# Forgetting attention in 11 steps per head pair instead of 14

## The reference, cut to what matters

```python
def forgetting_attention(q, k, v, logf):
    """logit[t,s] = q_t.k_s/sqrt(d) + sum_{s<j<=t} log f_j, causal."""
    c = jnp.cumsum(logf, axis=1)
    ...
        s = jnp.einsum("bthd,bshd->bhts", qi, k).astype(jnp.float32) * scale
        s = s + (cqi[..., :, None] - c_k[..., None, :])
        s = jnp.where(kpos[None, :] <= qpos[:, None], s, -jnp.inf)
        p = jax.nn.softmax(s, axis=-1).astype(v.dtype)
        return jnp.einsum("bhts,bshd->bthd", p, v)
```

## Time and profile before

| | |
|---|---|
| runs before | 2881.91, 2880.11, 2880.3 us; median 2880.3 |
| span of the profiled execution, first to last instruction | 2879.8 us (its own time is not told apart from the runs; the median lies 0.5 us above this span) |
| mean granted TensorE clock | 0.989 |
| busy: PE, DVE, ACT, POOL | 2752.2, 1715.2, 1046.7, 936.7 us |
| attention part, first projection matmul after the phase before to first matmul of the next phase | 893.2 to 1552.4 us |

### The profile page before, as it was taken

The page is one execution under the profiler, slowest core; times in us unless marked ns, Lnnn a source line. Parts: engine busy times, 40 slices in busy tenths (PEclk is TensorE's granted clock), DMA queues, the critical chain, the costliest instruction groups (busy, mean ns, idle before and its releaser), DMA issues. The chain is left out here.

```text
span 2879.8 us, 39468 instructions
## 1 busy us (share of the span) xinstructions
PE 2752.2 (96%) x15534; PEld 2109.5 (73%) x15534; DVE 1715.2 (60%) x2674; ACT 1046.7 (36%) x1735; POOL 936.7 (33%) x549
## 2 busy tenths in 40 slices
PE   6999999999999999999999999979999999998999
PEld 5979797977778677777776887756666666666777
DVE  5787878785121344444445113766776777777586
ACT  4342534343110233233334002335666654444232
POOL 2232323232564121121221333543221144332465
PEclk9999999999999999999999999999999999999999
DMA  4141423233533111101112223521101111113544
GB/s 167 56 89 66 85 69 85 75 76 119 195 117 106 42 53 45 49 30 52 52 45 107 103 81 141 176 94 44 47 19 44 37 41 34 41 41 101 201 149 110
DMA packets 113751, 236.53 MB, mean 82 GB/s; under 512 B 9120, under 2 KB 52896, under 8 KB 113568
## 3 DMA queue, kind: packets, MB, share of 16 engines
q1 hardware_dynamic: 63312, 172.14, 18.3%
q10 hardware_dynamic: 50256, 61.87, 7.4%
HBM read 189.88 MB, written 44.11 MB: 81 GB/s over the span
## 5 line engine op out<-in xcount | busy, mean ns | idle before, releaser
L79 PE MATMUL psum<-u_h,w_hi 128*128 128x512 f32 (+2 forms) x2624 | 1014.5, 387 | 22.6 <-DVE u_h L2903 6.1
L80 PE MATMUL psum<-u_h,w_hi 128*128 128x512 f32 (+2 forms) x2624 | 967.0, 369 | 0.0
L81 PE MATMUL psum<-u_h,w_lo 128*128 128x512 f32 (+2 forms) x2624 | 965.7, 368 | 0.0
L135 POOL TENSOR_SCALAR w_hi<-w_raw 128x1024 fp32r<-128x1024 f32 x212 | 241.8, 1141 | 1441.5 <-ACTq L1326 516.1
L79 PEld LDWEIGHTS psum<-u_h,w_hi 128*128 128x128 f32 x2624 | 496.8, 189 | 154.5 <-issue 69.0
L137 POOL TENSOR_TENSOR w_lo<-w_raw,w_hi 128x1024 fp32r<-128x1024 f32 x212 | 545.8, 2575 | 17.7
L80 PEld LDWEIGHTS psum<-u_h,w_hi 128*128 128x128 f32 x2624 | 497.1, 189 | 71.2 <-issue 11.5
L81 PEld LDWEIGHTS psum<-u_h,w_lo 128*128 128x128 f32 x2624 | 496.4, 189 | 70.8
L1351 ACT ACTIVATE f_exp<-psum 128x1024 f32<-128x1024 f32 (+4 forms) x112 | 82.1, 734 | 185.7 <-PE psum L1209 86.7
L2564 ACT ACTIVATE a_exp<-a_exp 128x1024 f32<-128x1024 f32 x96 | 101.5, 1057 | 126.5 <-DVE a_exp L2735 69.3
L1447 DVE CUSTOM_DVE_ANT_0 f_junk<-psum,f_decay,f_max 128x512 f32<-128x512 f32 (+2 forms) x96 | 60.3, 665 | 132.2 <-PE psum L1232 123.5
(11 more groups left out here) (431 smaller groups left out, 4424.6 us busy)
## 6 DMA issues: line engine op xcount, KB each, us to landing
w_raw<-in_w_all SPq DMA_DIRECT2D x212, 512.0 KB, 3.6
sums_rows<-s_acs ACTq DMA_DIRECT2D x32, 512.0 KB, 8.6
f_decay<-s_nc SPq DMA_DIRECT2D x16, 520.0 KB, 5.4
s_y<-conv_out ACTq DMA_DIRECT2D x16, 512.0 KB, 2.9
yo_raw<-s_y ACTq DMA_DIRECT2D x8, 1024.0 KB, 9.9
x_tok<-in_x SPq DMA_DIRECT2D x8, 512.0 KB, 8.3
s_xT<-xT SPq DMA_DIRECT2D x8, 512.0 KB, 4.9
s_pssd<-fox_last ACTq DMA_DIRECT2D x16, 256.0 KB, 2.2
```

The lines of the kernel that those rows point to most:

```text
L79: nc.tensor.matmul(out, w_hi[:, k], a_hi, start=(k == 0 and first), stop=False)
L80: nc.tensor.matmul(out, w_hi[:, k], a_lo, start=False, stop=False)
L81: return nc.tensor.matmul(out, w_lo[:, k], a_hi, start=False, stop=(k == kk - 1 and final))
L135: self.nc.gpsimd.tensor_scalar(self.hi[:, r], self.raw[:, r], 1.0, 1.0, ALU.mult, ALU.mult).then_inc(self.hi_done, 1)
```

## The change: what it does

Units near the diagonal share steps: (0, 3) with (0, 4), (1, 5) with (1, 8), and (1, 6) with (1, 7). A pair has 11 steps; `blocks(x)` lays the blocks of a step side by side in the same two banks, ending at column 512. Scores and values of a step do their blocks one after the other. An exp takes all blocks of 128 rows in one instruction and a block of 16 rows in another. DVE still adds block by block. The parts are spread anew (10 in steps 0 to 3, then 6, 6, 6, 6, 6, 5, 5), and so are maxima pieces, transposes and copies: the last pieces of a pair go to steps 0 and 1 (one may stand amid or behind the parts), its transposes to step 2, the next pair's pieces to steps 3 to 6 and 8 to 10.

```diff
-    units = [(0, kb) for kb in range(5)] + [(1, kb) for kb in range(9)]
-    NU = len(units)
+    units = [(0, [0]), (0, [1]), (0, [2]), (0, [3, 4])] + [(1, [kb]) for kb in range(5)] + [(1, [5, 8]), (1, [6, 7])]
+    NU, H1 = len(units), 4
...
+    def blocks(x):
+
+        h, kbs = units[x]
+        at, out = 512, []
+        for n, kb in enumerate(kbs):
+            width = 512 * h + 512 - first(h, kb)
+            at -= width
+            out.append((h, kb, rows(h, kb), first(h, kb), at, at + width))
+        return out
...
-    AT_STEP = {5: 0, 6: 1, 7: 2, 8: 3, 10: 4, 11: 5, 12: 6, 13: 7}
-    late_pieces = lambda p, x: {0: [4, 5], 1: [6, 7], 2: [8, 9]}.get(x, []) if p == 0 else [8 + x] if x < 2 else []
-    turn_step = lambda p: 3 if p == 0 else 2
+    AT_STEP = {3: 0, 4: 1, 5: 2, 6: 3, 8: 4, 9: 5, 10: 6}
+    late_pieces = lambda p, x: ({0: [4, 5, 6], 1: [7, 8, 9]} if p == 0 else {0: [7], 1: [8, 9]}).get(x, [])
+    TURN_LAST, TURN_NEXT = 2, 7
...
-    share = [head[8 * x:8 * x + 8] for x in range(5)]
-    for n in (4, 4, 4, 4, 4, 5, 6, 9, 0):
+    share = [head[10 * x:10 * x + 10] for x in range(4)]
+    for n in (6, 6, 6, 6, 6, 5, 5):
...
             def scores(p, r, x):
...
+                for h, kb, n, q0, at, end in blocks(x):
...
+                    st = score_bank(p, x) + at - q0
...
-                    for m in late_pieces(p, x)[:1]:
+                    late = late_pieces(p, x)
+                    for m in late[:1]:
                         maxima(p, r, m)
...
-                    for u, k in share_of(x, more):
+                    for n, (u, k) in enumerate(share_of(x, more)):
+                        if n == 5:
+                            for m in late[1:-1]:
+                                maxima(p, r, m)
                         part(p, r, u, k, more)
-                    for m in late_pieces(p, x)[1:]:
+                    if not share_of(x, more):
+                        for m in late[1:-1]:
+                            maxima(p, r, m)
+                    for m in late[1:][-1:]:
                         maxima(p, r, m)
                     values(p, x, more)
...
-                nc.scalar.activation(pt[0:n, x % 2, :, q0:512], src[:, :, q0:512], ACT.Exp, scale=0.125).then_inc(exp_ok, 1)
+                for n, a, e in [(P, full[-1][4], 512)] + [(META, b[4], b[5]) for b in bs if b[2] == META]:
+                    last = nc.scalar.activation(pt[0:n, (p * NU + x) % 2, :, a:e], src[0:n, :, a:e], ACT.Exp, scale=0.125)
+                last.then_inc(exp_ok, 1)
...
-                if x == 12:
+                if x == 10:
                     store(p, 0)
```

More of the change, by code:

```diff
@@ L1025, in fox_phase @@
     PAIRS = ATT_H // 2
[L1026 to L1027 removed]
+    units = [(0, [0]), (0, [1]), (0, [2]), (0, [3, 4])] + [(1, [kb]) for kb in range(5)] + [(1, [5, 8]), (1, [6, 7])]
+    NU, H1 = len(units), 4
     first = lambda h, kb: max(512 * h, P * kb - META)
     rows = lambda h, kb: META if kb == 4 + 4 * h else P
+    def blocks(x):
[6 more added lines that the diff above has]
+        return out
+    before = [sum(len(units[y][1]) for y in range(x)) for x in range(NU + 1)]
+    NB = before[NU]
+    gathered = lambda p, x: (p + 1) * NB + (before[x] if x >= 0 else before[NU + x] - NB)
     pieces = [[(0, 0, 144, 0), (1, 0, 272, 144)], [(2, 0, 400, 0), (3, 512, 528, 400)], [(3, 0, 512, 0)],
@@ L1205, in scores @@
[L1205 to L1210, removed]
+                for h, kb, n, q0, at, end in blocks(x):
+                    if n == META:
+                        pe.sem_inc(carried, 1)
+                    e = 512 * h + 512
+                    kc = slice(P * kb, P * kb + n)
+                    c0 = q0 - (P * kb - META)
+                    masked = c0 < n
+                    st = score_bank(p, x) + at - q0
+                    out = lambda j, a, b: ps[0:n, st + 512 * j + a:st + 512 * j + b]
+                    for t, (ka, qa) in enumerate([(k_hi, q_hi), (k_hi, q_lo), (k_lo, q_hi)]):
+                        for j in range(2):
+                            nc.tensor.matmul(out(j, q0, e), ka[64 * j:64 * j + 64, r, kc], qa[64 * j:64 * j + 64, r, q0:e], start=(t == 0), stop=False)
+                    for j in range(2):
+                        last = nc.tensor.matmul(out(j, q0, e), ek[64 * j:64 * j + 64, r, kc], eq[64 * j:64 * j + 64, q0:e], start=False, stop=not masked)
+                    if masked:
+                        for m in range(1 if n <= 64 else 2):
+                            d1 = min(64 * m + 64, n)
+                            for j in range(2):
+                                last = nc.tensor.matmul(out(j, q0, q0 + d1 - c0), K.halfid[64 * j:64 * j + 64, m, 0:n],
+                                                        K.maskq[64 * j:64 * j + 64, m, c0:d1], start=False, stop=(m == 1 or n <= 64))
@@ L1244, in values @@
             def values(p, x, more):
[L1245 to L1248, removed]
+                if units[x][1] == [0]:
+                    pe.wait_ge(o_ok, p * 2 + units[x][0] + 1)
                 if x == 0:
                     pe.wait_ge(proj_act, index(p - 1, G0) + 1)
-                if x in (4, 13):
-                    pe.wait_ge(proj_act, index(p, G1 if x == 4 else G2, more) + 1)
+                if x in (3, 9):
+                    pe.wait_ge(proj_act, index(p, G1 if x == 3 else G2, more) + 1)
                 pe.wait_ge(exp_ok, p * NU + x + 2)
-                for j in range(2):
-                    last = nc.tensor.matmul(ps[64 * j:64 * j + 64, OB + q0:OB + 512], V[0:n, kb, j],
-                                            pt[0:n, x % 2, j, q0:512], start=(kb == 0), stop=(kb == 4 + 4 * h))
+                for h, kb, n, q0, at, end in blocks(x):
+                    for j in range(2):
+                        last = nc.tensor.matmul(ps[64 * j:64 * j + 64, OB + q0 - 512 * h:OB + 512], V[0:n, kb, j],
+                                                pt[0:n, (p * NU + x) % 2, j, at:end], start=(kb == 0), stop=(kb == 4 + 3 * h))
                 last.then_inc(pv_ok, 1)
             def sums(p, h):
-                pe.wait_ge(acc_ok, p * NU + (5 if h == 0 else 14) + NU)
+                pe.wait_ge(acc_ok, gathered(p, H1 if h == 0 else NU))
                 pe.wait_ge(d_ok, p * 2 + h + 2)
@@ L1452, in accumulate @@
             def accumulate(p, x):
-                h, kb = units[x]
-                n, q0 = rows(h, kb), first(h, kb) - 512 * h
                 dve.wait_ge(exp_ok, p * NU + x + 2)
[L1456 to L1462, removed]
+                for m, (h, kb, n, q0, at, end) in enumerate(blocks(x)):
+                    to, src = acc[0:n, h, :, q0 - 512 * h:512], pt[0:n, (p * NU + x) % 2, :, at:end]
+                    if kb == 0:
+                        dve.wait_ge(sum_ok, p * 2 + h + 1)
+                        nc.vector.tensor_copy(to, src).then_inc(acc_ok, 1)
+                    else:
+                        dve.wait_ge(acc_ok, gathered(p, x) + m)
+                        nc.vector.tensor_tensor(to, to, src, ALU.add).then_inc(acc_ok, 1)
             def invert(p, h):
```

52 lines of the change are left out of this document (19 added, 33 removed).

## The result

The changed kernel takes 2888.5 us (median of 8 runs, 2883.1 to 2894.4) against 2881.6 of before on the same chip (8 runs, 2879.0 to 2883.4): ratio 1.0024, 95% interval 1.0016 to 1.0033. It is 6.9 us slower.

The account below looks back on a forecast made before the run. TensorE, busy 80.00 of 80.00 us mid-phase, was taken as the bound. Boundaries -3.5, turnaround +11.7, transposes +0.3, first pair -1.5, last pair -1.3 gave +5.7 on 2880.3: 2886.0 us, range 2881 to 2891, inner 2883.5 to 2888.5.

Parts of the forecast that it names:

- Turnaround: Step 0: Q1's first matmul waits for Q0's low part in the same PSUM bank; 1.67 us a pair, +11.7 in all.
- the rival that it is covered: Q0's low part is out before Q1's first matmul is due, leaving only the gains: 2874.3 us; chance 0.06.
- Boundaries: TensorE's changes between kinds of matmul that go with merged steps: 0.5 us less a pair, -3.5 over seven pairs.
- Decay lines: The next pair's lines, now needed in step 3, land in time with about 0.2 us of slack: cost 0.
- The rival's mechanism: Decay lines land late and hold TensorE, 0.7 us a pair, 4.9 in all: 2890.9 us; chance 0.12.
- Transposes: They may wait 0.05 us a pair for DVE's read of the last maxima piece: +0.3 in all.
- First pair: Waits for maxima shrink to one of 0.8 us at the ninth piece: 1.5 us less.
- Last pair: Of TensorE's three waits the first goes, the second stays, the third loses 0.6; with new waits and boundaries, 1.3 us less.
- The rival "savings only moved": The merged steps' changes between kinds of matmul are not saved but paid elsewhere: 2889.5 us; chance 0.09.
- The clock: Rival: a new wait in the first pair drops TensorE to the 1.2 GHz level, losing 5 us: 2891; chance 0.04.
- the prediction's own tests: Fails if Q1's idle time is absent, transposes or lines cost 0.5 us a pair, or period less turnaround is not 77.7.

Follow-up runs that it names:

- e3: The change with two buffers for the decay lines, issued early at the head of a pair's section: 3.0 us above before in both sets, ratios 1.0012 and 1.0007.
- e13: The change with parts spread 8, 12, 10, 10 and decay lines issued early in two buffers: ratio to before 0.9972, again 0.9983.
- e2: The kernel before, all 14 steps kept, with parts spread 10, 6, 8, 8, 8 so Q1 starts straight behind Q0: 2893.4 us, ratio 1.0043.
- e1: The change with parts spread 8, 12, 10, 10 instead of 10, 10, 10, 10, so Q1 begins in step 1: 2880.5 us, ratio 0.9995.
- e0: The change run again unaltered: 7.1 us above before, ratio 1.0024.
- e6: The kernel before with two buffers for the decay lines, issued early at the head of a pair's section: 0.4 us above before, ratio 0.9999.

## Why the prediction was right, and where by luck

The forecast of 2886.0 held to 2.5 us, and slower was the likelier side; but 2888.5 is the very edge of the forecast's inner range (2883.5 to 2888.5). Half of the miss is the base: the median of before was 2881.6 with more runs, not 2880.3. The sum of +5.7 stands against 6.4 in the first profile's part, 5.8 in the second's, and 6.9 and 7.1 by the medians. Term by term:

- *Turnaround*, 11.7: **right**. e3 less e13 is 79.15 - 77.45 = 1.70 a pair, e2 1.71 (1.67 predicted); seven make 11.9. Its place, its releaser and its seven times stood as forecast, and the rival that it is covered is out.
- *Boundaries*, -3.5: right in kind, too small. e13 less before is -0.82 a pair (-0.5 predicted, bound -0.9), seven make -5.7. The price of a run of parts was good. Adding up over six pairs of before and of e13 the distance from each matmul to the next start, by the kind of the first: the 240 parts of a pair lose 0.41 (two runs fewer, at 0.20 for first part and change to the values, were 0.40); scores, maxima pieces and masks lose 0.25, values 0.15. What I mis-sized were two smaller terms. The 0.2 that I charged for the last maxima piece does not show: the part ahead of it takes 0.25 us to the next start, ahead of values it is 0.27. And I left the price of a merged block's scores as it was, but values and the scores behind them give the 0.15. Without the one and with the other the sum would have been -0.87. In the timeline of the change, such a block starts right behind a mask:

```profile
1140.38 0.26 PE L1223 MATMUL psum<-maskq,halfid 64*128 64x64 bf16 x4
1140.44 0.20 PE L1216 MATMUL psum<-f_qhi,f_khi 64*16 64x16 f32 x2
```

- *Decay lines*, 0: **wrong**, and the step is "the slack is about 0.2 us. I take 0". The count of TensorE's work behind Q1 was right: from Q1's last matmul to the first product of step 3 it is 11.5 to 11.6 us in e3, where no line holds it, against 11.5. But I took 6.3 us, the latest landing of one profile, for the latest that there is; the lines need up to 7.6 in the change (7.9 in e1). The second issue goes out 5.1 us after Q1's last matmul, so it has 6.4 us. Lines just over that hold TensorE without an idle time of its own. In the timeline of the change that product starts at 1147.99, 11.7 after Q1's last matmul (1136.27) and 0.04 after a landing (1141.33 + 6.62), and only its weight load shows a wait; that period is 0.3 longer than e3's. (In this profile a weight load waits for the lines four times in all, the 1.57 among them, not four times more, as the expectation of e3 has it.) The rival's mechanism was true, at 2 to 4 us in all against the 4.9 of that rival.

```profile
1147.99 0.19 PEld L1241 LDWEIGHTS psum<-f_khi,f_qhi 64*128 64x128 f32 x2 [0.45 <-DMA f_decay<-s_nc]
1147.99 0.33 PE L1241 MATMUL psum<-f_khi,f_qhi 64*128 64x144 f32 x2
```

- *Transposes*, +0.3: nothing in the middle pairs; they start at the usual distance behind the mask.
- *First pair*, -1.5: about right. ACT's copy stands 0.33 us closer behind TensorE's work in the change, so I go here and in the last pair by TensorE's own starts, up to the transposes of v that follow a pair's last values (1039.14 before, 1038.57 now). From V0's first matmul it is 107.8 us in both profiles; less +1.70 and -0.82 that leaves -0.9. But the two are not alike. In every profile TensorE's granted clock falls to 0.50 in this stretch, for 10.2 us in some (before, e0, e3) and 13.7 us in others (the change, e6, the second of e3), and two profiles of one kernel that differ in this differ by 0.7 to 0.8 us here. Like with like the term is -1.5 (the change against e6) and -1.7 (e3 against before). The wait that I named, at the ninth piece, stands at 979.92 with 0.93 (0.8 predicted).
- *Last pair*, -1.3: 1.5 less by these starts (42.1 instead of 43.6), and the waits alone are 1.5 less. The terms were mixed: 0.49 for the last piece as said, no 0.3 for copied maxima, but 0.50 for the sums; the second wait, which was to stay, fell from 1.90 to 1.18, and nothing is left that would be the boundaries' 0.5.

So +5.7 came out near 6.4 because boundaries were 2.2 better and lines 2.1 to 2.7 worse than I had put them: two errors that cancel, and that they did is luck. The rival "savings only moved" is out (e13). The clock did not fall behind a turnaround in any kernel; behind a late line it did once (e1). By the prediction's own tests, the lines come near its bound of 0.5 us a pair (0.4 a period in the two profiles, 0.6 a pair by the medians, so past it by the one and not by the other), and the period less the turnaround is 77.45 where 77.7 was given, so the boundary term failed its test.

## What to carry to other kernels

Merging steps pays only as far as what it puts side by side is not coupled: the same change gives -0.3% once its parts are cut at the end of a unit that shares its bank with the next, a shared buffer is doubled, and one read is put ahead on another engine. Before parts are spread anew, list which unit uses which bank, and keep other work of the turnaround's length (here 1.8 us) between the last matmul of one and the first of the next. A transfer that has been moved nearer to its use needs the slack of its worst landing, and one profile need not show that one: before's had 6.3 us, and others with the old order of steps 7.3 and 7.9.

## What the runs showed of the hardware that was not expected

In the middle pairs the same two transfers landed after 4.9 to 7.9 us, over all profiles. In the change and in e1 the slowest came right behind an issue that took SP 1.05 and 0.75 us instead of 0.43, but in e0 and e6 one of 7.5 and one of 7.9 came behind issues of 0.43, and in e6 an issue of 1.35 landed after 6.2; why is open. Two waits of like length on TensorE had different ends: after 1.62 us in e1 the granted clock was 0.66 in the window behind it and the pair lost 3.4 us, after 1.57 us in the change it stayed at 1.00 (windows of the change) and the pair lost 1.8. That too is open; the waits of 1.41 in the middle pairs never lowered it.

```profile
1465.00:1470.00 5.00, 3.43 (x30) 3.09 (x29) 2.24 (x11) 1.48 (x2) 0.00 (x0) 1.00 0.06 24
1470.00:1475.00 5.00, 5.00 (x46) 4.13 (x45) 0.68 (x3) 1.81 (x3) 2.21 (x2) 1.00 0.15 56
```
